# Two of eight K steps in the seven-product form, and GpSimd forming their sums of weights

## The chip, the cores and the metric

The kernel runs on one core of one Trainium2 chip. The metric is the device time of one launch in microseconds (us). An engine's name stands for its instruction stream: PE is TensorE, DVE is VectorE, ACT is ScalarE, POOL is GpSimd, SP is the queue that issues the loads.

## What is computed

One decoder block in float32 for 256 rows of 2048 columns: a projection, an mLSTM branch and a convolution branch, their gated merge, a residual, and then a feed-forward network (FFN) with its residual and a last norm. The change touches the FFN's first half:

```python
hf = rmsnorm(x, norm_ffn[l])
act = silu(einsum('bsd,df->bsf', hf, w_gate[l])) * einsum('bsd,df->bsf', hf, w_up[l])
x = x + einsum('bsf,fd->bsd', act, w_down[l])
```

`w_gate` and `w_up` are 2048 x 5632.

## The kernel before

Float32 accuracy on PE comes from splitting: each factor is a high part (ACT rounds it to fp32r) and a low part (DVE subtracts the high part from the raw value), and each product is three matmuls, high by high, low by high, high by low. One matmul has 128 x 128 stationary and 512 moving columns.

Weights pass through a ring: SP loads a chunk of 1 MB into one of 4 slots of `w_raw`; ACT writes `w_hi` (2 slots), DVE writes `w_lo` (2 slots), PE multiplies. SP reloads a slot when DVE has written the `w_lo` of the chunk four back (`lo_split`). ACT may write `w_hi` of chunk c when PE has ended the high products of chunk c-2 (`hi_used`); DVE may write `w_lo` when PE has ended chunk c-2 (`lo_used`).

**The FFN's gate and up** (`ffn_turn`, `pair_step`, `pair_split`) run over 11 blocks of 512 columns, one turn each. A turn has 8 K steps. A step takes four 128 x 512 tiles of weights, two of gate and two of up, which lie two K tiles apart, and two row blocks by two K tiles of the normed x. A plain step (small "s" in `STEPS`) is 8 products, 24 matmuls. A step in the seven-product form (capital "S"), a Strassen-like scheme, is 7 products, 21 matmuls, and needs three sums of weights beside the raw ones and sums of x tiles. The sums of x (`form_raw`, `form_hi`, `form_lo`) are made once, by `forms` on DVE; the sums of weights are made in each S step:

```python
V.tensor_tensor(t_raw[:, 0:2, :], raw[:, 0:1, :].to_broadcast([P, 2, COLS]), raw[:, 1:3, :], ALU.add)
V.tensor_tensor(raw[:, 0, :], t_raw[:, 0, :], raw[:, 2, :], ALU.add)
V.tensor_tensor(t_raw[:, 2, :], raw[:, 0, :], raw[:, 3, :], ALU.add)
```

(L1146, L1149, L1151). Then ACT makes `t_hi` (128 x 1536) and `w_hi` (the second sum lies in the raw slot, so `w_hi` waits for it too), DVE makes `t_lo` (L1153) and `w_lo` (L858). `t_raw`, `t_hi` and `t_lo` have one buffer each.

The order is written out by hand in each engine's stream. During step j ACT and DVE prepare step j+1 (`pair_split(j + 1)`); the preparation of the next turn's step 0 comes in step 7. Steps 0 and 7 need both parts at their start, since they go bank by bank; the others need `w_lo` after their high products. At `LAST_S` three PSUM banks are complete: ACT copies one (`c_gate`), DVE adds the others (L1224, L1226). After step 7's `pair_split` DVE runs five adds from PSUM (L1235), ACT two silus (L779), DVE two multiplications (L1249); `turn_act` transposes the result after steps 1 and 2 of the next turn, and ACT copies it out (`act_taken`). In turn 0 some work is extra: the last block of x is transposed, split (`f_high`, `f_low`) and made into sums.

In the stage before, the output projection, `forms(0, ...)` is made in its last block's step q = 1, and the first S step's sums in q = 3. `form_raw0` lies where `t_raw` lies, so the sums of weights wait for `form_lo`. After the FFN's 11 turns comes the down projection (L1668 to L1675).

GpSimd has little to do before: constants, copies of heads (L452, L454), and reciprocal roots in two operations each, with a pow (L430, L433).

Of the kernel before, what the change touches and what calls it, by code (L numbers as in the profile page):

```python
# [29 lines left out]
ALU = mybir.AluOpType  # L30
# [5 lines left out]
P = 128  # L36
# [44 lines left out]
def hybrid_block(nc, x, norm_mix, w_in, b_igate, b_fgate, conv_w, mh_norm, w_branch_a, w_branch_b,  # L81
# [51 lines left out]
    with ExitStack() as ctx:  # L133
# [36 lines left out]
        x1 = at("x1", [P, RT, D], F32, R2 + AT)  # L170
        FORMS = 22
        HALF_CH = 3 * COLS * 4
# [51 lines left out]
        f_raw[3] = at("f_raw3", [P, KB, SEQ], F32, Z + 2 * AT)  # L224
        form_raw1 = at("form_raw1", [P, 10, P], F32, Z)

# [186 lines left out]
        def _(pool):  # L413
# [48 lines left out]
            pool.wait_ge(h_squared, RT * H)  # L462
            rstd_of(h_mean, ss[:], ss[:], rstd[:], 1, DV, h_rstd)
            pool.wait_ge(x1_summed, 1)
            rstd_of(x1_mean, sums[:], sums[:], r_x[:, 1, :], 1, D, x1_rstd)
            for r in range(RT):
                pool.wait_ge(y_total, r + 1)
                rstd_of(y_mean, sums[:, r:r + 1], ssx[:, 1, r:r + 1], r_x[:, 0, r:r + 1], r + 1, D, y_rstd)

        @block.scalar  # L470
        def _(act):
# [258 lines left out]

            def f_high(b, turned, halves=1):

                for h in range(halves):
                    act.wait_ge(f_turned, turned + h)
                    ks = range(h * KB // halves, (h + 1) * KB // halves)
                    src = bank_kt(4) if halves == 1 else ps[:, B_FREE, :].rearrange("p (k t) -> p k t", k=2)
                    for k in ks:
                        c = V_FN + b * KB + k
                        last = copy(f_raw[b][:, k, :], src[:, k - ks[0], :], scale=vecT[:, c:c + 1])
                    last.then_inc(f_raw_done, 1)  # L740
                    act.wait_ge(f_raw_done, turned + h)
                    copy(fT_hi[:, b * KB + ks[0]:b * KB + ks[-1] + 1, :],
                         f_raw[b][:, ks[0]:ks[-1] + 1, :]).then_inc(f_hi_done, 1)

            def forms_high(g, raw, at_form, count):
                act.wait_ge(form_step, 5 * (g + 1))
                copy(form_hi[:, at_form:at_form + count, :], raw[:]).then_inc(form_hi_done, 1)

            for n in range(NB):
                for q in range(BC):  # L750
                    c = Chunk(G_OUT + n * BC + q)
                    if n == NB - 1 and q == BC - 1:
                        pair_split(0, 0)
# [28 lines left out]
            def ffn_turn(i, last=False):  # L782
                first = starts(i)
                for j in range(2 * BC):
                    if j < 2 * BC - 1:
                        pair_split(j + 1, i)
                    elif last:
                        split(Chunk(G_DOWN))
                    else:
                        pair_split(0, i + 1)  # L790
                    if j == 0:
                        if first:
                            f_high(NB - 1, NB, halves=2)
# [11 lines left out]
                    if last and j == LAST_S + 1:  # L805
# [44 lines left out]
        def _(dve):  # L850
# [279 lines left out]

            raw_units = w_raw[:].rearrange("p s (u n) -> p s u n", u=4)

            def pair_split(j, i):
# [12 lines left out]
                V.tensor_tensor(t_raw[:, 0:2, :], raw[:, 0:1, :].to_broadcast([P, 2, COLS]), raw[:, 1:3, :],  # L1146
                                ALU.add).then_inc(t_step, 1)
                dve.wait_ge(t_step, before * T_STEPS + 1)
                V.tensor_tensor(raw[:, 0, :], t_raw[:, 0, :], raw[:, 2, :], ALU.add).then_inc(t_step, 1)  # L1149
                dve.wait_ge(t_step, before * T_STEPS + 2)  # L1150
                V.tensor_tensor(t_raw[:, 2, :], raw[:, 0, :], raw[:, 3, :], ALU.add).then_inc(t_step, 1)  # L1151
                dve.wait_ge(t_hi_done, before + 1)
# [32 lines left out]
            for n in range(NB):  # L1185
                for q in range(BC):
# [18 lines left out]
            def ffn_turn(i, last=False):  # L1205
                first = starts(i)
                for j in range(2 * BC):
# [98 lines left out]
        def _(pe):  # L1306
# [262 lines left out]
            def tile_of(part, c, name):  # L1569
# [192 lines left out]
```

## Time and profile before

| | us |
|---|---|
| median of 2 runs | 1812.46 (1812.35 to 1812.58) |
| the profiled execution | 1813.08 |
| its span in the trace | 1811.3 |
| PE busy in it | 1750.6 |
| DVE busy | 1056.2 |
| ACT busy | 807.3 |
| POOL busy | 31.1 |

The profiled execution is 0.6 us above the median, and its span is 1.8 us short of its own time (launch and end). A busy share is an average over the stages; the FFN's gate and up lie between 1025 and 1560 us of the span.

### The profile page before, as it was taken

The numbers are of one execution on the slowest core, as the hardware profiler recorded it, in microseconds if no ns is written. First come the engines' busy times: TensorE is split into PE (matmuls) and PEld (weight loads), VectorE is DVE, ScalarE is ACT, GpSimd is POOL, SyncE is SP. The second block draws the span as 40 slices with busy tenths as digits, with TensorE's granted clock in tenths as the row PEclk, the third lists the DMA queues.
The fourth block names the chain that finished last, engine by engine and source line by source line (L and its number), as shares of the span: only waits on it lengthen the run. The fifth ranks groups of instructions, "written<-read, shape, count | busy, mean of one in ns | idle before, by whom it ended". The sixth has DMA issues, their size and how long they took to land.

```text
span 1811.3 us, 21190 instructions
## 1 busy us (share of the span) xinstructions
PE 1750.6 (97%) x7784; PEld 1441.7 (80%) x7784; DVE 1056.2 (58%) x862; ACT 807.3 (45%) x717; POOL 31.1 (2%) x43
## 2 busy tenths in 40 slices
PE   9999999999999999999999889999999999999997
PEld 8888888888888888888888667777777777788886
DVE  5454445655565544444445587777777777654455
ACT  6344445454444433333335444444444444544444
POOL 1000010110000000000000000000000000000000
PEclk9999999999999999999999999999999999999999
DMA  8656555555565555565665345555545555655552
GB/s 288 199 165 200 167 177 168 173 163 185 162 205 188 188 186 192 179 208 174 201 238 188 128 149 176 185 175 173 173 162 174 185 180 170 226 189 188 201 190 93
DMA packets 152106, 331.09 MB, mean 183 GB/s; under 512 B 8736, under 2 KB 8832, under 8 KB 146048
## 3 DMA queue, kind: packets, MB, share of 16 engines
q1 hardware_dynamic: 152064, 330.51, 55.0%
q8 instruction: 29, 0.48, 0.1%
q14 instruction: 13, 0.11, 0.0%
HBM read 328.38 MB, written 2.10 MB: 182 GB/s over the span
## 4 chain that ended last, share of the span: by engine, by line
PE 77%; DVE 8%; ACT 7%; issue 7%; DVEq 0%; ACTq 0%; DMA 0%; POOL 0%; SPq 0%; POOLq 0%
PE ps L1321 17%; PE ps L1322 17%; PE ps L1330 17%; ACT w_hi L472 7%; PE ps L1668 4%; PE ps L1675 4%; PE ps L1670 4%; PE ps L1598 3%; PE ps L1599 3%; PE ps L1603 3%; DVE w_lo L858 3%; DVE t_raw L1146 2%; DVE w_raw L1149 1%; DVE t_raw L1151 1%; PE ps L1339 1%
## 5 line engine op out<-in xcount | busy, mean ns | idle before, releaser
L858 DVE TENSOR_TENSOR w_lo<-w_raw,w_hi 128x2048 fp32r<-128x2048 f32 x308 | 706.7, 2299 | 469.6 <-ACT w_hi L472 466.0
L472 ACT ACTIVATE w_hi<-w_raw 128x2048 fp32r<-128x2048 f32 (+1 forms) x309 | 587.5, 1907 | 383.6 <-PE ps L1322 214.0
L1321 PE MATMUL ps<-w_hi,xT_hi 128*128 128x512 f32 x1024 | 404.4, 395 | 0.0
L1322 PE MATMUL ps<-w_hi,xT_lo 128*128 128x512 f32 x1024 | 398.7, 389 | 0.0
L1330 PE MATMUL ps<-w_lo,xT_hi 128*128 128x512 f32 x1024 | 253.0, 389 | 0.0
L1330 PEld LDWEIGHTS ps<-w_lo,xT_hi 128*128 128x128 f32 x1024 | 192.2, 188 | 39.9
L1321 PEld LDWEIGHTS ps<-w_hi,xT_hi 128*128 128x128 f32 x1024 | 192.3, 188 | 39.7
L1322 PEld LDWEIGHTS ps<-w_hi,xT_lo 128*128 128x128 f32 x1024 | 192.3, 188 | 39.0
L1598 PE MATMUL ps<-w_hi,fT_hi 128*128 128x512 f32 x396 | 162.3, 410 | 47.1 <-DVE w_lo L858 30.9
L1599 PE MATMUL ps<-w_hi,fT_lo 128*128 128x512 f32 x396 | 157.6, 398 | 0.0
L1598 PEld LDWEIGHTS ps<-w_hi,fT_hi 128*128 128x128 f32 x396 | 75.9, 192 | 71.5 <-issue 49.5
L1603 PE MATMUL ps<-w_lo,fT_hi 128*128 128x512 f32 x396 | 122.8, 396 | 0.0
L472 ACT ACTIVATE t_hi<-t_raw 128x1536 fp32r<-128x1536 f32 x33 | 49.2, 1489 | 116.7 <-DVE t_raw L1151 115.5
L1668 PE MATMUL ps<-w_hi,a_hi 128*128 128x512 f32 x352 | 96.1, 390 | 0.7 <-ACT actT L472 0.7
L1670 PE MATMUL ps<-w_hi,a_lo 128*128 128x512 f32 x352 | 95.9, 389 | 0.0
L1675 PE MATMUL ps<-w_lo,a_hi 128*128 128x512 f32 x352 | 88.9, 390 | 0.0
L1153 DVE TENSOR_TENSOR t_lo<-t_raw,t_hi 128x1536 fp32r<-128x1536 f32 x33 | 58.0, 1758 | 52.8 <-ACT t_hi L472 52.8
L1603 PEld LDWEIGHTS ps<-w_lo,fT_hi 128*128 128x128 f32 x396 | 75.9, 192 | 16.1
L1599 PEld LDWEIGHTS ps<-w_hi,fT_lo 128*128 128x128 f32 x396 | 76.3, 193 | 14.3
L1668 PEld LDWEIGHTS ps<-w_hi,a_hi 128*128 128x128 f32 x352 | 66.0, 188 | 14.9 <-ACT actT L472 0.9
L1675 PEld LDWEIGHTS ps<-w_lo,a_hi 128*128 128x128 f32 x352 | 66.0, 188 | 14.1 <-DVE w_lo L858 0.5
L1670 PEld LDWEIGHTS ps<-w_hi,a_lo 128*128 128x128 f32 x352 | 66.0, 188 | 13.7
(220 smaller groups left out, 1792.2 us busy)
## 6 DMA issues: line engine op xcount, KB each, us to landing
w_raw<-in_w_in SPq DMA_DIRECT2D x127, 1024.0 KB, 5.5
w_raw<-in_w_gate SPq DMA_DIRECT2D x88, 512.0 KB, 3.6
w_raw<-in_w_up SPq DMA_DIRECT2D x88, 512.0 KB, 4.4
w_raw<-in_w_down SPq DMA_DIRECT2D x44, 1024.0 KB, 4.8
w_raw<-in_w_branch_a SPq DMA_DIRECT2D x16, 1024.0 KB, 5.1
w_raw<-in_w_branch_b SPq DMA_DIRECT2D x16, 1024.0 KB, 5.0
w_raw<-in_w_out SPq DMA_DIRECT2D x16, 1024.0 KB, 5.2
xn<-in_x SPq DMA_DIRECT2D x4, 512.0 KB, 8.4
```

The costliest lines, as they stand in the source:

```text
L472: copy = lambda o, i, **kw: nc.scalar.activation(o, i, ACT.Copy, **kw)
L858: V.tensor_tensor(w_lo[:, chunk.split, :], w_raw[:, chunk.raw, :], w_hi[:, chunk.split, :].bitcast(F32), ALU.subtract).then_inc(lo_split, 1)
L1153: V.tensor_tensor(t_lo[:], t_raw[:].rearrange("p u n -> p (u n)"), t_hi[:].bitcast(F32), ALU.subtract).then_inc(t_lo_done, 1)
L1321: T.matmul(ps[:, banks + r, :], rows(hi, k, r), w, start=(q == 0 and k == 0), stop=False)
L1322: last = T.matmul(ps[:, banks + r, :], rows(lo, k, r), w, start=False, stop=False)
L1330: last = T.matmul(ps[:, banks + r, :], rows(hi, k, r), w, start=False, stop=(q == BC - 1 and k == KB - 1))
L1598: T.matmul(ps[:, bank, :], tile_of(0, k, name), moving(0, u), start=start, stop=False)
L1599: return T.matmul(ps[:, bank, :], tile_of(1, k, name), moving(0, u), start=False, stop=False)
L1603: return T.matmul(ps[:, bank, :], tile_of(0, k, name), moving(1, u), start=False, stop=stop)
L1668: T.matmul(ps[:, 4 * r + n, :], tile(h, r), cols_of(w_hi, n), start=start, stop=False)
L1670: ins = T.matmul(ps[:, 4 * r + n, :], tile(l, r), cols_of(w_hi, n), start=False, stop=False)
L1675: ins = T.matmul(ps[:, 4 * r + n, :], tile(h, r), cols_of(w_lo, n), start=False, stop=stop)
```

## The change

`STEPS` has two S steps, 0 and 3, where there were three, 0, 3 and 5. K pairs 4 and 5 keep their natural order. The three sums of weights move from DVE to POOL, into a loop that runs over the S steps by itself and waits for the landed pair and for the `t_lo` of the S step before. For x, the second group needs no S1, S2 and S4 forms, so `forms(1, ...)` makes 8 tiles and not 10; the split of the forms is a function of its own, one step later than the sums, for both groups. In turn 0 the two halves of the last block are split in steps 0 and 1, and not both in step 0. `LAST_S` is 3: ACT's copy of `c_gate` comes in step 3 and DVE's two adds in step 4.

```diff
-STEPS = "SssSsSss"
-PAIR_OF = (0, 2, 3, 1, 5, 4, 6, 7)
-LAST_S = 5
+STEPS = "SssSssss"
+PAIR_OF = (0, 2, 3, 1, 4, 5, 6, 7)
+LAST_S = 3
@@ POOL
+            def weight_sums(j, i):
+                c = Chunk(G_FFN + j, i, 2 * BC)
+                before = S_BEFORE[j] + i * S_TURNS
+                raw = raw_units[:, c.raw]
+                pool.wait_ge(pair_landed[c.raw], 32 * (j // RAW_SLOTS + 1) + i * 64)
+                if starts(i) and j == 0:
+                    pool.wait_ge(form_lo_done, 1)
+                else:
+                    pool.wait_ge(t_lo_done, before)
+                nc.gpsimd.tensor_tensor(out=t_raw[:, 0:2, :], in0=raw[:, 0:1, :].to_broadcast([P, 2, COLS]),
+                                        in1=raw[:, 1:3, :], op=ALU.add).then_inc(t_step, 1)
+                pool.wait_ge(t_step, before * T_STEPS + 1)
+                nc.gpsimd.tensor_tensor(out=raw[:, 0, :], in0=t_raw[:, 0, :], in1=raw[:, 2, :],
+                                        op=ALU.add).then_inc(t_step, 1)
+                pool.wait_ge(t_step, before * T_STEPS + 2)
+                nc.gpsimd.tensor_tensor(out=t_raw[:, 2, :], in0=raw[:, 0, :], in1=raw[:, 3, :],
+                                        op=ALU.add).then_inc(t_step, 1)
+            weight_sums(0, 0)
             pool.wait_ge(x1_summed, 1)
             rstd_of(x1_mean, sums[:], sums[:], r_x[:, 1, :], 1, D, x1_rstd)
+            weight_sums(LAST_S, 0)
+            with pool.Fori(1, FB) as i:
+                for j in (0, LAST_S):
+                    weight_sums(j, i)
@@ ACT
-                    if n == NB - 1 and q == 1:
+                    if n == NB - 1 and q == 2:
                         forms_high(0, form_raw0, 0, 12)
...
-                    if j == 0:
-                        if first:
-                            f_high(NB - 1, NB, halves=2)
-                        else:
-                            silu(i - 1, 1)
+                    if first and j in (0, 1):
+                        f_high(NB - 1, NB, 2, j)
+                    if not first and j == 0:
+                        silu(i - 1, 1)
...
-                        forms_high(1, form_raw1, 12, 10)
+                        forms_high(1, form_raw1, 12, 8)
@@ DVE, pair_split
-                raw = raw_units[:, c.raw]
-                dve.wait_ge(pair_landed[c.raw], 32 * (j // RAW_SLOTS + 1) + i * 64)
-                if starts(i) and j == 0:
-                    dve.wait_ge(form_lo_done, 1)
-                else:
-                    dve.wait_ge(t_lo_done, before)
-                V.tensor_tensor(t_raw[:, 0:2, :], ...)
-                V.tensor_tensor(raw[:, 0, :], ...)
-                V.tensor_tensor(t_raw[:, 2, :], ...)
                 dve.wait_ge(t_hi_done, before + 1)
@@ DVE, streams
                     if n == NB - 1 and q == 1:
-                        forms(0, form_raw0, 0, 2)
+                        forms(0, form_raw0, 2)
+                    if n == NB - 1 and q == 2:
+                        forms_low(0, form_raw0, 0, 12)
...
-                        f_low(NB - 1, NB, halves=2)
+                    if first and j in (0, 1):
+                        f_low(NB - 1, NB, 2, j)
+                    if first and j == 1:
+                        forms(1, form_raw1, KB)
                     if first and j == 2:
-                        forms(1, form_raw1, 12, 3)
-                    if j == LAST_S:
+                        forms_low(1, form_raw1, 12, 8)
+                    if j == LAST_S + 1:
                         dve.wait_ge(p1_out, i + 1)
```

## Rows read from the trace of the kernel before

**Rows 1.** The page's part 1: busy time, share and instructions of each engine.

```profile
PE 1750.6 (97%) x7784; PEld 1441.7 (80%) x7784; DVE 1056.2 (58%) x862; ACT 807.3 (45%) x717; POOL 31.1 (2%) x43
```

**Rows 2.** Windows: stretch, length, busy of PE, PEld, DVE, ACT, POOL; PEclk, DMA, GB/s.

```profile
1200.00:1300.00 100.00, 93.24 (x402) 75.59 (x402) 76.61 (x60) 45.42 (x33) 0.00 (x0) 0.97 0.52 178
...
1600.00:1700.00 100.00, 100.00 (x443) 82.81 (x442) 48.84 (x37) 42.79 (x38) 0.00 (x0) 1.00 0.55 196
```

**Rows 3.** Timeline, PE: first matmuls of turns 0, 1, 4 and 10, then the down projection's.

```profile
1025.16 0.77 PE L1598 MATMUL ps<-w_hi,fT_hi 128*128 128x512 f32 x1 [4.91 <-DVE w_lo L858]
...
1084.11 0.49 PE L1598 MATMUL ps<-w_hi,fT_hi 128*128 128x512 f32 x1 [2.37 <-DVE w_lo L858]
...
1228.16 0.79 PE L1598 MATMUL ps<-w_hi,fT_hi 128*128 128x512 f32 x1 [2.63 <-DVE w_lo L858]
...
1515.19 0.79 PE L1598 MATMUL ps<-w_hi,fT_hi 128*128 128x512 f32 x1 [2.63 <-DVE w_lo L858]
...
1560.01 0.61 PE L1668 MATMUL ps<-w_hi,a_hi 128*128 128x512 f32 x2
```

**Rows 4.** Timeline, PE: after step 0 of turn 0; first matmuls of two following steps.

```profile
1032.32 0.60 PE L1559 MATMUL ps<-ident,x 128*128 128x128 f32 x4
1032.67 0.48 PE L1598 MATMUL ps<-w_hi,fT_hi 128*128 128x512 f32 x1
...
1214.49 0.39 PE L1598 MATMUL ps<-w_hi,fT_hi 128*128 128x512 f32 x1
...
1219.93 0.39 PE L1598 MATMUL ps<-w_hi,fT_hi 128*128 128x512 f32 x1
```

**Rows 5.** Timeline: `c_gate`'s copy, then the preparation of turn 4's step 0.

```profile
1214.77 0.60 ACT L472 ACTIVATE c_gate<-ps 128x512 f32<-128x512 f32 x1 [3.51 <-PE ps L1603]
...
1222.21 1.49 ACT L472 ACTIVATE t_hi<-t_raw 128x1536 fp32r<-128x1536 f32 x1 [5.04 <-DVE t_raw L1151]
...
1223.60 1.90 ACT L472 ACTIVATE w_hi<-w_raw 128x2048 fp32r<-128x2048 f32 x1
1223.73 1.76 DVE L1153 TENSOR_TENSOR t_lo<-t_raw,t_hi 128x1536 fp32r<-128x1536 f32 x1 [1.64 <-ACT t_hi L472]
...
1225.62 2.29 DVE L858 TENSOR_TENSOR w_lo<-w_raw,w_hi 128x2048 fp32r<-128x2048 f32 x1
```

**Rows 6.** Groups of instructions, 1025 to 1560 us: count, busy us, mean ns, idle before.

```profile
L858 DVE TENSOR_TENSOR w_lo<-w_raw,w_hi 128x2048 fp32r<-128x2048 f32 x89 | 203.0, 2291 | 47.5 <-ACT w_hi L472 45.2
...
L1146 DVE TENSOR_TENSOR t_raw<-w_raw 128x1024 f32<-128x1024 f32 x32 | 39.0, 1219 | 0.0
...
L1149 DVE TENSOR_TENSOR w_raw<-t_raw,w_raw 128x512 f32<-128x512 f32 x32 | 22.2, 693 | 1.1
...
L1235 DVE TENSOR_TENSOR c_up<-ps,c_up 128x512 f32<-128x512 f32 x22 | 15.0, 682 | 0.0
L1249 DVE SCALAR_TENSOR_TENSOR c_up<-c_up,r_x,c_gate 128x512 f32<-128x512 f32 x20 | 15.0, 748 | 3.6 <-ACT c_gate L779 3.6
```

**Rows 7.** Groups of instructions, POOL, whole span: the pow of 16 columns.

```profile
L433 POOL TENSOR_TENSOR rstd<-ss,half 128x16 f32<-128x16 f32 x1 | 2.9, 2916 | 0.1
```

**Rows 8.** Timeline, DVE and then POOL, around 244 us.

```profile
244.37 2.59 DVE L858 TENSOR_TENSOR w_lo<-w_raw,w_hi 128x2048 fp32r<-128x2048 f32 x1 [0.35 <-ACT w_hi L472]
...
244.21 0.61 POOL L452 COPY head_qk<-qk 128x512 f32 x1 [49.93 <-DVE vx L1008]
244.76 2.26 POOL L454 COPY head_cols<-cols 128x6 f32 x1
```

**Rows 9.** The page's DMA issues: KB each, median us from issue to landing.

```profile
w_raw<-in_w_up SPq DMA_DIRECT2D x88, 512.0 KB, 4.4
```

**Rows 10.** Timeline: the end of the output projection, before turn 0.

```profile
1011.18 1.49 ACT L472 ACTIVATE form_hi<-form_raw 128x1536 fp32r<-128x1536 f32 x1 [4.30 <-DVE form_raw L1178]
...
1012.70 1.76 DVE L1181 TENSOR_TENSOR form_lo<-form_raw,form_hi 128x1536 fp32r<-128x1536 f32 x1 [1.55 <-ACT form_hi L472]
...
1014.52 0.50 PE L1321 MATMUL ps<-w_hi,mT_hi 128*128 128x512 f32 x1 [1.23 <-ACT w_hi L472]
```

More of the change, by code:

```diff
@@ L170, in hybrid_block @@
         x1 = at("x1", [P, RT, D], F32, R2 + AT)
-        FORMS = 22
+        FORMS = 20
         HALF_CH = 3 * COLS * 4
@@ L224, in hybrid_block @@
         f_raw[3] = at("f_raw3", [P, KB, SEQ], F32, Z + 2 * AT)
-        form_raw1 = at("form_raw1", [P, 10, P], F32, Z)
+        form_raw1 = at("form_raw1", [P, 8, P], F32, Z)
         g_final = at("g_final", [P, D], F32, R3)
@@ L309, in hybrid_block @@
         T_STEPS = 3
+        FORM_STEPS = (0, 5, 7)
         F_BLOCKS = NB - 1
@@ L463, in _ @@
             rstd_of(h_mean, ss[:], ss[:], rstd[:], 1, DV, h_rstd)
+            raw_units = w_raw[:].rearrange("p s (u n) -> p s u n", u=4)
+            def weight_sums(j, i):
[16 more added lines that the diff above has]
+            weight_sums(0, 0)
             pool.wait_ge(x1_summed, 1)
             rstd_of(x1_mean, sums[:], sums[:], r_x[:, 1, :], 1, D, x1_rstd)
+            weight_sums(LAST_S, 0)
+            with pool.Fori(1, FB) as i:
+                for j in (0, LAST_S):
+                    weight_sums(j, i)
             for r in range(RT):
@@ L729, in pair_split, with f_high @@
                 split(c, (t_step, before * T_STEPS + T_STEPS))
-            def f_high(b, turned, halves=1):
-                for h in range(halves):
+            def f_high(b, turned, halves=1, at_half=0):
+                for h in (range(at_half, at_half + 1) if halves > 1 else (0,)):
                     act.wait_ge(f_turned, turned + h)
@@ L745, in forms_high @@
             def forms_high(g, raw, at_form, count):
-                act.wait_ge(form_step, 5 * (g + 1))
+                act.wait_ge(form_step, FORM_STEPS[g + 1])
                 copy(form_hi[:, at_form:at_form + count, :], raw[:]).then_inc(form_hi_done, 1)
@@ L804, in ffn_turn @@
                         copy(c_gate[:, 0, :], ps[:, B_P1, :]).then_inc(p1_out, 1)
-                    if last and j == LAST_S + 1:
+                    if last and j == LAST_S + 2:
                         stage(Chunk(G_DOWN))
@@ L1128, in _ @@
                 merge_turn(i)
-            raw_units = w_raw[:].rearrange("p s (u n) -> p s u n", u=4)
             def pair_split(j, i):
@@ L1139, in pair_split @@
                 before = S_BEFORE[j] + i * S_TURNS
-                raw = raw_units[:, c.raw]
-                dve.wait_ge(pair_landed[c.raw], 32 * (j // RAW_SLOTS + 1) + i * 64)
-                if starts(i) and j == 0:
-                    dve.wait_ge(form_lo_done, 1)
-                else:
-                    dve.wait_ge(t_lo_done, before)
[L1146 to L1151, printed above, removed]
                 dve.wait_ge(t_hi_done, before + 1)
@@ L1155, in pair_split, with f_low @@
                 split(c)
-            def f_low(b, done, halves=1):
-                for h in range(halves):
+            def f_low(b, done, halves=1, at_half=0):
+                for h in (range(at_half, at_half + 1) if halves > 1 else (0,)):
                     dve.wait_ge(f_hi_done, done + h)
@@ L1163, in f_low, with forms @@
                                     ALU.subtract).then_inc(f_lo_done, 1)
-            def forms(g, raw, at_form, plain):
+            def forms(g, raw, plain):
                 a, b = f_raw[g], f_raw[g + 2]
@@ L1170, in forms, with forms_low @@
                 top, low = slice(0, P), slice(P, 2 * P)
-                V.tensor_tensor(s1, a[:, 0:sums, low], b[:, 0:sums, low], ALU.subtract).then_inc(form_step, 1)
+                if sums:
+                    V.tensor_tensor(s1, a[:, 0:sums, low], b[:, 0:sums, low], ALU.subtract).then_inc(form_step, 1)
                 V.tensor_tensor(raw[:, 0:KB, :], a[:, :, top], a[:, :, low], ALU.subtract).then_inc(form_step, 1)
-                dve.wait_ge(form_step, 5 * g + 1)
-                V.tensor_tensor(s2, s1, a[:, 0:sums, top], ALU.subtract).then_inc(form_step, 1)
+                if sums:
+                    dve.wait_ge(form_step, FORM_STEPS[g] + 1)
+                    V.tensor_tensor(s2, s1, a[:, 0:sums, top], ALU.subtract).then_inc(form_step, 1)
                 V.tensor_tensor(raw[:, KB:KB + plain, :], b[:, sums:, top], b[:, sums:, low],
                                 ALU.subtract).then_inc(form_step, 1)
-                dve.wait_ge(form_step, 5 * g + 3)
-                V.tensor_tensor(s4, s2, b[:, 0:sums, top], ALU.add).then_inc(form_step, 1)
+                if sums:
+                    dve.wait_ge(form_step, FORM_STEPS[g] + 3)
+                    V.tensor_tensor(s4, s2, b[:, 0:sums, top], ALU.add).then_inc(form_step, 1)
+            def forms_low(g, raw, at_form, count):
                 dve.wait_ge(form_hi_done, g + 1)
-                count = KB + plain + 3 * sums
                 V.tensor_tensor(form_lo[:, at_form:at_form + count, :], raw[:],
@@ L1226, in ffn_turn @@
                         V.tensor_tensor(c_gate[:, 1, :], ps[:, B_P7, :], c_up[:, 0, :], ALU.add).then_inc(u_step, 1)
-                    if last and j == LAST_S + 1:
+                    if last and j == LAST_S + 2:
                         stage(Chunk(G_DOWN))
@@ L1575, in tile_of @@
                 g, k = c // KB, c % KB
-                plain = (2, 3)[g]
+                plain = (2, 4)[g]
                 sums = KB - plain
```

## Prediction

> **What bounds the kernel now.** I read the page's shares first: PE is busy for 97% of the span [rows 1], so time can be won only where PE waits or runs slowly. The windows say where: in the down projection 100 us hold 443 matmuls at a granted clock of 1.00; in the FFN's gate and up, 402 at 0.97 [rows 2]. Then the timeline of PE, for the turns. Turn 0 takes 1084.11 - 1025.16 = 58.95 us, turns 1 to 9 take (1515.19 - 1084.11) / 9 = 47.90 us each, turn 10 takes 1560.01 - 1515.19 = 44.82 us [rows 3].
>
> Against this, PE's own pace: a plain step of 24 matmuls takes 1219.93 - 1214.49 = 5.44 us, 0.2267 us a matmul [rows 4]. An S step is then 4.76 us. Transposes between two steps cost about 0.5 us: 0.35 until the next step starts, the rest in its long first matmul [rows 4]. A turn of before holds 3 x 21 + 5 x 24 = 183 matmuls: 41.5 + 1.0 = 42.5 us. So some 5.4 us of each 47.90 are lost. The reader sees where in rows 3 and 5: PE stands 2.63 us at the turn's start, for a `w_lo` that is the last of a serial chain. DVE forms three sums (1.22 + 0.69 + 0.69) [rows 6], ACT makes `t_hi`, then `w_hi`, DVE `t_lo` and at last `w_lo`. DVE does the sums only after the `w_lo` before, and ACT idles 5.04 us for them [rows 5]. The remainder is a second short stall at the other S steps and the clock, which after the turn's stall is granted at its lower level, 1.2 in place of 2.4 GHz; step 0 of turn 0, behind 4.91 us of idleness, took 1032.32 - 1025.16 = 7.16 us and not 4.76 [rows 3, 4].
>
> **PE's new work.** One S step becomes plain: 3 matmuls more a turn, 0.68 us, 7.5 us over 11 turns. All of it is on the path. A turn's floor is 186 x 0.2267 + 1.0 = 43.17 us.
>
> **What leaves DVE.** Nine additions a turn (3 x 2.6 = 7.8 us) and one `t_lo` (1.76). ACT loses one `t_hi` (1.49). Left on DVE are 8 x 2.29 + 2 x 1.76 + 5 x 0.68 + 2 x 0.69 + 2 x 0.75 = 28.1 us of 43.17 [rows 5, 6].
>
> **What comes to POOL.** Two-input adds of 1024, 512 and 512 columns, twice a turn. No row shows one. From below, DVE's 2.6 us for a step. The nearest row of POOL is a copy of 512 columns, 0.61 us [rows 8]; 2048 columns are 2.4 us with one input, 4.9 with two read one after the other. The only two-input rows are pows, 2.9 us for 16 columns [rows 7], which as a rate would make a step over 300 us; it is a different operation, and the copy is nearest in size and kind. I take 4.9 us (2.45 + 1.2 + 1.2).
>
> What POOL does also takes from DVE. A copy of POOL runs from 244.21 to 244.82 [rows 8], and the `w_lo` that starts in it takes 2.59 and not 2.29 us; the tiny copy behind it, 6 columns, lasts 2.26 us and ends at 247.02, with that `w_lo` at 246.96. So the two exclude each other, an instruction at a time. The Trainium skill says the same (SBUF — State Buffer, section on the two separate sides): the pair of ports is an exclusive lock between a GpSimd operation and a DVE one with two SBUF inputs, and the first to start holds it. By that rule the L1235 adds, with one input in PSUM, go free. Its GPSIMD Engine Reference (section 3.1) gives 4497 ns for a two-input add of 2048 columns and advises DVE for such adds; by it a step is an estimated 4.8 us, and the sum below stays.
>
> **Does the new chain fit in 43.17 us?** Time 0 is the start of a turn's step 0 on PE. Steps start at 0, 4.76, 10.70, 16.64, 21.40, 26.84, 32.28, 37.72, and the next turn's at 43.17.
> - ACT copies `c_gate` at 21.4 (0.60) [rows 5]. `w_lo`(4) waits for `w_hi`(4), which comes behind the transposed result's copy at 16.7, and ends at 21.5. SP then issues the load of the next step 0; gate's and up's issue take some 0.6 us, and up lands 4.4 later [rows 9], at 26.5.
> - POOL's first add: 26.6 to 29.05. `w_lo`(6), ready at 27.8, waits for it and ends at 31.35. The second add then to 32.65, `w_lo`(7) to 34.95, the third add to 36.2.
> - `t_hi` 36.3 to 37.8, `t_lo` to 39.75, `w_hi` to 39.6, `w_lo`(next 0) 39.8 to 42.1. PE wants it at 43.17: 1.05 us to spare.
> - The load of step 3's pair is issued at 35.1 and lands at 40.0; POOL waits for the `w_lo` under way, then adds from 42.15 to about 47.5, between DVE's two multiplications. The next `w_lo`(1) ends about 50.5, 7.3 after the new turn's start, and is wanted at 4.76 + 3.63 = 8.4. One us to spare.
> - What is queued behind POOL's waits: only its own later sums and, in turn 0, the reciprocal root, in which DVE's and ACT's last steps of turn 0 take an interest, 40 us later.
>
> So the gain rests on about 1 us of cover in two places. Gone that, each us late costs one us a turn.
>
> **Entry and turn 0.** The forms' split one step later frees ACT for `w_hi` of the output projection's last chunk, and the 1.23 us stall at 1014.52 goes [rows 10]. But DVE now does that chunk's `w_lo` first (1011.15 to 1013.4), then `form_lo` to 1015.2; POOL adds 1015.3 to 1020.2 and the chain of rows 5 follows: `t_hi` to 21.8, `t_lo` to 23.6, `w_lo` to 26.0. Turn 0 starts at 1026.1 and not 1025.16: +0.95. In turn 0 the split of the second half no longer stands ahead of `w_hi`(2); `w_hi`(3) ends at 44.8 for a start at 45.2, `form_lo` at 48.7 for one at 50. I find no stall, so 43.17 + 2.4 (low clock in step 0) = 45.57.
>
> **The sum**
> - entry: +0.95
> - turn 0: 45.57 - 58.95 = -13.4
> - turns 1 to 9: 9 x (43.17 - 47.90) = -42.6
> - turn 10: 43.17 - 44.82 = -1.65
> - all: -56.7 us. Profiled execution 1813.08 to 1756.4; on the median of 1812.46, 1755.8. I say 1756.
>
> With POOL at DVE's price only the entry moves, by -2.3: 1753.5.
>
> **Rivals**
> 1. *POOL takes the lock before the turn's last `w_lo`.* Step 3's adds are released by `t_lo` (39.75) and the landing (40.0), `w_lo` is ready at 39.8. If the pair lands a few tenths sooner, POOL may be first; `w_lo` ends at 42.2 + 2.3 = 44.6, 1.5 us late, in ten turns 15: 1771. For: 0.2 us between the two. Against: DVE follows itself at once.
> 2. *POOL also holds up DVE's adds from PSUM.* No row excludes it. Adds and POOL's would alternate from 42.1 on: the three adds that free the first two shared banks end near 49.0, PE wants the second of these banks at 43.17 + 12 x 0.2267 = 45.9. Some 3 us a turn, 30 in all: 1786. The Trainium skill's lock rule, quoted above, speaks against this one.
> 3. *POOL's two-input add is slow, and the kernel slower.* The chain above allows x <= 6.1 us for a step's sums (43.17 - 26.6 - 4.6 of two `w_lo` - 5.9 of the chain after). Above, each us is a us a turn: 8.1 gives 1776, 10.8 brings back 47.9, from 15.4 on the kernel is over 2% slower. At 16 us (2.0 for 512 columns of one input, over three times the copy's): 1756 + 10 x 9.9 = 1855. For: the pow of rows 7. Against: the copy of rows 8.
>
> **How the numbers follow.** Forecast (1750 to 1764) 0.52; rival 1 (1764 to 1776) 0.22; rival 2 (1776 to 1795) 0.14; POOL so slow, or a chain of late steps, that time ends between 1776 and 1849 by other ways 0.08; rival 3 above 1849 0.04. A change of 2%, 36 us, is about what a measurement of this kernel can tell from none. Faster by over 2% is below 1776: 0.52 + 0.22 + 0.02 for the low side of the others = 0.76. Slower 0.04, same 0.20. Range: 1750, below POOL's lower bound, to 1782, the lower part of rival 2. The likeliest case's own range is 1750 to 1764.
>
> **What the profile after would show.** Turn starts 43.2 us apart, without the 2.63 us stall; granted clock 0.99 or 1.00 in this stage; POOL at some 22 x 4.9 = 108 us plus what it waits in the lock; `w_lo` with a mean above 2.29 us, up to 3.5 for the ones behind POOL. Turn starts 44.7 apart with a wait for `w_lo` is rival 1; a wait for `c_step`'s adds, with L1235 longer than 0.68, is rival 2; ACT's `t_hi` waiting for POOL past 38 us of the turn is rival 3. I am wrong most cheaply in the price of POOL's add and in the order in which the lock is granted.

## The result and the profile after

| | before | changed |
|---|---|---|
| median, us | 1812.46 | 1755.84 (1755.32 to 1756.35) |
| profiled execution, us | 1813.08 | 1755.32 |
| its span, us | 1811.3 | 1753.5 |

The ratio is 0.9688, with a 95% interval of 0.9665 to 0.9712. A second set of runs gave 1756.33 and 0.9685 (0.9669 to 0.9701). So the change saves 3.1%, and the prediction's 1756 and its 56.7 us stand.

The page's part 1 of the changed kernel answers to [rows 1]:

```profile
PE 1732.6 (99%) x7817; PEld 1434.9 (82%) x7817; DVE 995.3 (57%) x749; ACT 794.2 (45%) x706; POOL 173.3 (10%) x109
```

Two windows of the changed kernel, with the columns of [rows 2], lie in the FFN's gate and up, and the last in the down projection:

```profile
1200.00:1300.00 100.00, 100.00 (x453) 82.73 (x452) 70.78 (x44) 48.73 (x36) 32.00 (x15) 1.00 0.57 196
1300.00:1400.00 100.00, 100.00 (x452) 82.79 (x451) 72.38 (x44) 50.08 (x36) 24.91 (x13) 1.00 0.55 189
...
1600.00:1700.00 100.00, 100.00 (x443) 82.81 (x442) 47.28 (x36) 43.50 (x37) 0.00 (x0) 1.00 0.53 193
```

There are 33 more matmuls and yet 18 us less of PE busy time: at the higher clock they take less, and 100 us of the gate and up now hold some 452 matmuls at a granted clock of 1.00, where there were 402 at 0.97. The timeline of PE of the changed kernel shows the starts of turns 0 and 1 and of the down projection (it answers to [rows 3]), and the end of step 0 of turn 0:

```profile
1025.76 0.76 PE L1619 MATMUL ps<-w_hi,fT_hi 128*128 128x512 f32 x1 [7.30 <-DVE w_lo L884]
...
1032.04 0.60 PE L1580 MATMUL ps<-ident,x 128*128 128x128 f32 x4
...
1070.95 0.39 PE L1619 MATMUL ps<-w_hi,fT_hi 128*128 128x512 f32 x1
...
1502.21 0.61 PE L1689 MATMUL ps<-w_hi,a_hi 128*128 128x512 f32 x2
```

Turn 0 takes 45.19 us, the ten others (1502.21 - 1070.95) / 10 = 43.13. The one long stall left in this stage is the first, 7.30 us.

One turn's start in POOL's and then DVE's timeline (turn 5 starts on PE at 1243.45). The first three POOL rows are the sums for its step 0, the last three those for its step 3. L884 is `w_lo`, L1165 `t_lo`, L1256 the adds from PSUM, L1270 the two multiplications:

```profile
1227.28 2.40 POOL L477 TENSOR_TENSOR t_raw<-w_raw 128x1024 f32<-128x1024 f32 x1 [23.37 <-DMA w_raw<-in_w_up]
1229.76 3.23 POOL L480 TENSOR_TENSOR w_raw<-t_raw,w_raw 128x512 f32<-128x512 f32 x1
1233.07 3.29 POOL L483 TENSOR_TENSOR t_raw<-w_raw 128x512 f32<-128x512 f32 x1
1240.36 4.18 POOL L477 TENSOR_TENSOR t_raw<-w_raw 128x1024 f32<-128x1024 f32 x1 [4.00 <-DMA w_raw<-in_w_up]
1244.62 1.28 POOL L480 TENSOR_TENSOR w_raw<-t_raw,w_raw 128x512 f32<-128x512 f32 x1
1245.98 1.62 POOL L483 TENSOR_TENSOR t_raw<-w_raw 128x512 f32<-128x512 f32 x1
...
1227.94 3.88 DVE L884 TENSOR_TENSOR w_lo<-w_raw,w_hi 128x2048 fp32r<-128x2048 f32 x1
1232.91 2.29 DVE L884 TENSOR_TENSOR w_lo<-w_raw,w_hi 128x2048 fp32r<-128x2048 f32 x1 [1.09 <-ACT w_hi L499]
1238.08 1.76 DVE L1165 TENSOR_TENSOR t_lo<-t_raw,t_hi 128x1536 fp32r<-128x1536 f32 x1 [2.88 <-ACT t_hi L499]
1239.97 2.29 DVE L884 TENSOR_TENSOR w_lo<-w_raw,w_hi 128x2048 fp32r<-128x2048 f32 x1
...
1244.58 0.68 DVE L1256 TENSOR_TENSOR c_gate<-ps,c_gate 128x512 f32<-128x512 f32 x1
1245.18 2.98 DVE L1270 SCALAR_TENSOR_TENSOR c_up<-c_up,r_x,c_gate 128x512 f32<-128x512 f32 x2
```

The exclusion of [rows 8] is at work in most of these rows. POOL's first add ends at 1229.68, and the `w_lo` that began beside it needs 3.88 us, until 1231.82. POOL's second add needs 3.23, since it waits for that `w_lo`; the third needs 3.29, since it waits for the `w_lo` of 1232.91. But the L1256 add, which reads PSUM and one SBUF tile, keeps its 0.68 us beside the POOL add of 1244.62. A length in these rows contains the wait for the other engine. Free of it, POOL's adds take 2.40 and 1.28 us. The chain ends when `w_lo` of step 0 does, at 1242.26, 1.19 us before PE wants it.

This turn is one of the two tight ones in this trace. In the other eight POOL's third add starts a few hundredths ahead of `w_lo`(7), and not behind it; `w_lo` of step 0 then ends 2.72 us before PE wants it. So it is for turn 4, which starts on PE at 1200.33 (POOL, then DVE):

```profile
1189.73 1.29 POOL L483 TENSOR_TENSOR t_raw<-w_raw 128x512 f32<-128x512 f32 x1
1189.78 3.38 DVE L884 TENSOR_TENSOR w_lo<-w_raw,w_hi 128x2048 fp32r<-128x2048 f32 x1 [1.29 <-ACT w_hi L499]
...
1195.32 2.29 DVE L884 TENSOR_TENSOR w_lo<-w_raw,w_hi 128x2048 fp32r<-128x2048 f32 x1 [0.48 <-ACT w_hi L499]
```

In the trace of `changed_again`, the same kernel, all ten turns are of the tight kind, with 0.98 to 1.19 us to spare. Either way a turn takes 43.13 us.

### The profile page after: what moved, and what is told of

Read it like the earlier page. It is cut to its first block, busy times and chain, and to the rows that moved or that the text cites. A ratio compares the mean times of both kernels' runs of the same rounds, so it can differ in the third digit from the quotient of the medians.

```text
span 1753.5 us, 21136 instructions
## 1 busy us (share of the span) xinstructions
PE 1732.6 (99%) x7817; PEld 1434.9 (82%) x7817; DVE 995.3 (57%) x749; ACT 794.2 (45%) x706; POOL 173.3 (10%) x109
## 4 chain that ended last, share of the span: by engine, by line
PE 96%; DVE 1%; POOL 1%; ACT 1%; issue 0%; DMA 0%; SPq 0%; DVEq 0%; POOLq 0%; ACTq 0%
PE ps L1342 18%; PE ps L1343 18%; PE ps L1351 18%; PE ps L1619 9%; PE ps L1620 9%; PE ps L1624 9%; PE ps L1689 4%; PE ps L1696 4%; PE ps L1691 4%; PE ps L1360 1%; PE ps L1580 1%; ACT w_hi L499 0%; DVE w_lo L884 0%; POOL t_raw L477 0%; DMA w_raw<-in_w_in 0%
## 5 line engine op out<-in xcount | busy, mean ns | idle before, releaser
L884 DVE TENSOR_TENSOR w_lo<-w_raw,w_hi 128x2048 fp32r<-128x2048 f32 x308 | 732.8, 2381 | 500.9 <-ACT w_hi L499 498.9
L1619 PE MATMUL ps<-w_hi,fT_hi 128*128 128x512 f32 x440 | 173.8, 395 | 7.6 <-DVE w_lo L884 7.3
L1620 PE MATMUL ps<-w_hi,fT_lo 128*128 128x512 f32 x440 | 171.7, 390 | 0.0
L477 POOL TENSOR_TENSOR t_raw<-w_raw 128x1024 f32<-128x1024 f32 x22 | 56.1, 2552 | 821.4 <-DVE form_lo L1197 532.8
L1624 PE MATMUL ps<-w_lo,fT_hi 128*128 128x512 f32 x440 | 130.4, 390 | 0.0
L1619 PEld LDWEIGHTS ps<-w_hi,fT_hi 128*128 128x128 f32 x440 | 82.7, 188 | 24.8 <-issue 7.7
L1624 PEld LDWEIGHTS ps<-w_lo,fT_hi 128*128 128x128 f32 x440 | 82.7, 188 | 17.2
L1620 PEld LDWEIGHTS ps<-w_hi,fT_lo 128*128 128x128 f32 x440 | 82.8, 188 | 16.5
L1619 PE MATMUL ps<-w_hi,form_hi 128*128 128x512 f32 x176 | 68.9, 391 | 0.0
```

The source lines that it names most:

```text
L477: nc.gpsimd.tensor_tensor(out=t_raw[:, 0:2, :], in0=raw[:, 0:1, :].to_broadcast([P, 2, COLS]), in1=raw[:, 1:3, :], op=ALU.add).then_inc(t_ ...
L884: V.tensor_tensor(w_lo[:, chunk.split, :], w_raw[:, chunk.raw, :], w_hi[:, chunk.split, :].bitcast(F32), ALU.subtract).then_inc(lo_split, 1)
L1619: T.matmul(ps[:, bank, :], tile_of(0, k, name), moving(0, u), start=start, stop=False)
L1620: return T.matmul(ps[:, bank, :], tile_of(1, k, name), moving(0, u), start=False, stop=False)
L1624: return T.matmul(ps[:, bank, :], tile_of(0, k, name), moving(1, u), start=False, stop=stop)
```

## Experiments

**Who forms the sums, and where the last S step stands.** Four kernels with two S steps (the changed kernel is one of them): sums on DVE or POOL, second S step at 3 or at 5. And one with only half the change, three S steps with POOL.

`two_s_dve`, against the changed kernel:

```diff
@@ DVE, pair_split
+                V.tensor_tensor(t_raw[:, 0:2, :], raw[:, 0:1, :].to_broadcast([P, 2, COLS]), raw[:, 1:3, :], ALU.add)
+                V.tensor_tensor(raw[:, 0, :], t_raw[:, 0, :], raw[:, 2, :], ALU.add)
+                V.tensor_tensor(t_raw[:, 2, :], raw[:, 0, :], raw[:, 3, :], ALU.add)
                 dve.wait_ge(t_hi_done, before + 1)
@@ POOL
-            weight_sums(0, 0)
...
```

> The changed kernel with its two S steps, but DVE forms the sums of weights as before (2.6 us a step). Theory A (what made the old chain late was ACT's copy of c_gate at step 5, which held w_hi(7) back, and the S step there; POOL is not needed): w_lo(7) ends at 34.8 of the turn, sums to 37.5, t_hi to 39.1, t_lo to 41.0, w_lo(next 0) to 43.3 against a start wanted at 43.17, so 0 to 0.3 us of stall a turn, and the entry 2.3 us shorter: 1753 to 1759. Rival B (the move to POOL carries the gain): a stall of 2 us or more at each turn's start with the low clock behind it, some 3 us a turn: 1780 to 1790.

Measured: 1764.91 us, ratio 0.9732 (0.9716 to 0.9748). Theory A's mechanism, not its size. Turns 1 to 10 take 43.57 us on average, 0.44 above the changed kernel's, 4.4 us together. The entry, counted from the first of the `forms` additions, is 2.4 us shorter, as expected. The miss is in turn 0, which I had not looked at: it takes 51.70 us and not 45.19. In its timeline PE waits 3.95 us before step 3, since ACT's `t_hi` waits 4.55 us for sums which stand in DVE's stream behind `f_low` and `forms`, and eleven matmuls after that wait start 0.43 us apart.

```profile
1024.29 0.47 PE L1608 MATMUL ps<-w_hi,fT_hi 128*128 128x512 f32 x1 [4.85 <-DVE w_lo L859]
1046.72 0.79 PE L1608 MATMUL ps<-w_hi,fT_hi 128*128 128x512 f32 x1 [3.95 <-ACT w_hi L474]
```

`late_s_dve` and `late_s_pool`, against `two_s_dve` and the changed kernel:

```diff
-STEPS = "SssSssss"
-PAIR_OF = (0, 2, 3, 1, 4, 5, 6, 7)
-LAST_S = 3
+STEPS = "SssssSss"
+PAIR_OF = (0, 2, 3, 4, 5, 1, 6, 7)
+LAST_S = 5
@@ PE, turn 0: the second group's forms are wanted a step sooner
-                    if first and j == KB:
+                    if first and j == KB - 1:
```

> As two_s_dve (two S steps, DVE forms the sums), but the second S step is step 5 and LAST_S is 5, as in the kernel before; the K pairs 1, 4 and 5 change places for it. Same matmuls as the changed kernel. Theory A (the old turn start was late because ACT's copy of c_gate at the end of step 5 stands ahead of w_hi(7)): w_hi(7) ends at 34.7 and not 32.4 of the turn, w_lo(next 0) at 45.6, 2.4 us late, and the low clock behind it, 4 us a turn more than two_s_dve: 1795 to 1810. Rival (the gain of two_s_dve came from fewer sums on DVE as such): as two_s_dve, 1762 to 1770.

> The changed kernel (POOL forms the sums) with the second S step at 5 in the same way. Theory A: the sums are ready on POOL before the late w_hi(7) is, so the chain after it is only t_hi, t_lo and w_lo, and ends 0.5 to 1 us ahead: 1756 to 1764. So POOL takes away the harm of the late copy, and moving the copy takes away the need of POOL. Rival (the lock makes POOL's sums late): a stall at the turn's start, 1775 or more.

Measured: `late_s_dve` 1819.06 us, ratio 1.0033 (1.0020 to 1.0045), about the time of the kernel before. `late_s_pool` 1762.59 us, ratio 0.9723 (0.9707 to 0.9739). The timeline of `late_s_dve` (ACT, DVE, PE) shows a chain like the old one:

```profile
1208.54 0.60 ACT L474 ACTIVATE c_gate<-ps 128x512 f32<-128x512 f32 x1 [3.51 <-PE ps L1613]
1209.03 1.91 ACT L474 ACTIVATE w_hi<-w_raw 128x2048 fp32r<-128x2048 f32 x1
...
1210.97 2.29 DVE L859 TENSOR_TENSOR w_lo<-w_raw,w_hi 128x2048 fp32r<-128x2048 f32 x1 [3.22 <-ACT w_hi L474]
1213.18 0.68 DVE L1234 TENSOR_TENSOR c_up<-ps,c_gate 128x512 f32<-128x512 f32 x1
1213.90 0.69 DVE L1236 TENSOR_TENSOR c_gate<-ps,c_up 128x512 f32<-128x512 f32 x1
1214.51 1.22 DVE L1147 TENSOR_TENSOR t_raw<-w_raw 128x1024 f32<-128x1024 f32 x1
...
1223.18 0.77 PE L1608 MATMUL ps<-w_hi,fT_hi 128*128 128x512 f32 x1 [3.88 <-DVE w_lo L859]
```

ACT waits 3.51 us for step 5's end to copy `c_gate`, and `w_hi`(7) stands behind that copy; then `w_lo`(7), two adds and only then the sums. PE waits 3.88 us at each turn's start, and turns 1 to 9 take 49.5 us on average. That is 9 us more than the top of my range, in which I had left out the two adds between `w_lo`(7) and the sums: from the end of `w_lo`(7), 1213.26, to the sums at 1214.51 they cost 1.25 us a turn.

These two adds are not in the old chain. In the kernel before they come at step `LAST_S` itself, while ACT makes `w_hi`(7); the changed kernel has them at `LAST_S` + 1, and `late_s_dve` took that over. The kernel before, at the same place of turn 3:

```profile
1215.26 1.91 ACT L472 ACTIVATE w_hi<-w_raw 128x2048 fp32r<-128x2048 f32 x1
...
1215.49 0.70 DVE L1224 TENSOR_TENSOR c_up<-ps,c_gate 128x512 f32<-128x512 f32 x1 [1.51 <-ACT c_gate L472]
1216.22 0.69 DVE L1226 TENSOR_TENSOR c_gate<-ps,c_up 128x512 f32<-128x512 f32 x1
1217.21 2.29 DVE L858 TENSOR_TENSOR w_lo<-w_raw,w_hi 128x2048 fp32r<-128x2048 f32 x1 [0.29 <-ACT w_hi L472]
1219.41 1.22 DVE L1146 TENSOR_TENSOR t_raw<-w_raw 128x1024 f32<-128x1024 f32 x1
```

So of the 3.88 us of stall in `late_s_dve` some 1.25 are that kernel's own, and the rest is close to the 2.63 us of the kernel before. An estimate from these rows: with the two adds in their old place `late_s_dve` would be some 13 us faster, near 1806 us. No run shows it.

In `late_s_pool` a turn is 43.13 us, as in the changed kernel: POOL has the sums ready while `w_hi`(7) is late. Turn 0 takes 6.6 us more, 51.82: a 3.93 us stall before step 3, which the earlier want of the forms brings (the second group's `form_lo` ends at 1048.98, PE goes on at 1049.08), and the low clock behind it. So with two S steps each half of the remedy is nearly enough alone: the S step at 3 lets DVE do the sums, POOL makes the late S step harmless. Of the 63 us between 1819.1 and 1756.3 the one gives 54, the other 56; they don't add. By the estimate above some 13 us of each are the misplaced adds. The position of the S step, of the copy and of the two adds were moved together in these runs, so what the copy alone is worth was not measured. From the rows, `w_hi`(7) starts 14.15 us before the next turn does in `late_s_dve`, with 3.88 of stall in it, so 10.27 us before PE wants it; in `two_s_dve` it is 12.84 - 0.18 = 12.66 us. The late copy thus takes 2.4 us of the chain, and the adds 1.25: together nearly the 3.70 us by which the two stalls differ.

`three_s_pool`, against the kernel before: the three additions leave DVE's `pair_split`, and POOL has `weight_sums` with

```diff
+            weight_sums(0, 0)
...
+            for j in (3, 5):
+                weight_sums(j, 0)
+            with pool.Fori(1, FB) as i:
+                for j in (0, 3, 5):
+                    weight_sums(j, i)
```

> The kernel before with its three S steps and its LAST_S of 5; only the sums of weights move to POOL. Its PE floor is 42.5 us a turn. Theory A: POOL's adds come off DVE, w_lo(7) ends at 36.4, the sums by 36.3, w_lo(next 0) at about 42.0 of 42.5, so the turn is near its floor, 42.5 to 43.5; turn 0 keeps its long order (53 us or so) and the entry grows by 2.3 us: 1755 to 1767. Rival B (three S steps are too many for POOL with one t_raw and the lock): a turn of 44.5 us or more, 1775 and above.

Measured: 1785.86 us, ratio 0.9848 (0.9832 to 0.9865): rival B. A turn is 45.1 us. POOL's timeline, the sums of step 5 of one turn and of step 0 of the next:

```profile
1233.65 4.55 POOL L476 TENSOR_TENSOR t_raw<-w_raw 128x1024 f32<-128x1024 f32 x1 [9.86 <-DVE t_lo L1166]
1238.28 3.33 POOL L479 TENSOR_TENSOR w_raw<-t_raw,w_raw 128x512 f32<-128x512 f32 x1
1241.68 1.28 POOL L482 TENSOR_TENSOR t_raw<-w_raw 128x512 f32<-128x512 f32 x1
1246.44 4.50 POOL L476 TENSOR_TENSOR t_raw<-w_raw 128x1024 f32<-128x1024 f32 x1 [3.47 <-DVE t_lo L1166]
```

Before these two steps POOL waits for `t_lo`, that is for the single `t_raw`, and not for a landing as in the changed kernel. And the sums need 5 us alone, but take 9.3 in step 5 (two of the three adds wait in the lock), 11.3 in step 0 (all three) and 7.1 in step 3. With two S steps in the same late order (`late_s_pool`) a turn is at its floor, so it is the third S step that costs, by its wait for the buffer and its turns in the lock; the two were not told apart.

**How much cover there is.** POOL adds of 128x512 into a spare tile ahead of each step's sums; the results stay whole:

```diff
+                for m in range(N):
+                    nc.gpsimd.tensor_tensor(out=spare[:], in0=raw[:, 1, :], in1=raw[:, 3, :], op=ALU.add)
```

> One more POOL add of 128x512 ahead of each step's sums, 1.37 us. w_lo of step 0 has 1.2 us to spare in the changed kernel. Theory: 0.2 us late a turn if POOL doesn't take the lock before it, 1757 to 1760; with the lock's 1.1 us as in extra2, 1768 to 1772.

> The changed kernel with two more POOL adds of 128x512 into a spare tile ahead of each S step's sums: 2.7 us longer on POOL. In the trace of the changed kernel w_lo(0) ends 1.2 us before PE wants it. Theory (the sums on POOL lie on the chain, with about 1.2 us of cover): 1.5 us late a turn, 1768 to 1774. Rival (POOL is hidden, PE alone bounds): 1756.

> The same with four more POOL adds, 5.4 us longer. Theory: 4.2 us late a turn and the low clock after such a stall, 0 to 1.8 us more: 1798 to 1816, about the time of the kernel before. Rival (hidden): 1756.

Measured, one run each: 1772.02, 1801.83 and 1845.34 us. Turns 1 to 9 take 44.4, 47.1 and 50.9 us on average. That POOL lies on the chain is shown; that a us late costs a us is not: `extra2` and `extra4` came out 28 and 29 us above my ranges, and `extra1` reached its upper range in another way than the one I named (its `w_lo` of step 0 keeps its 2.29 us). With 1.37, 2.7 and 5.4 us more on POOL in each S step, a turn loses 1.3, 4.0 and 7.8 us.

In `extra1` most of it is lost at the second place of cover that the prediction names, the `w_lo` of step 1. Turn 4 starts at 1208.81; the low products of its step 1 come 9.16 us later, and not 8.39 as in the changed kernel:

```profile
1217.97 1.21 PE L1630 MATMUL ps<-w_lo,fT_hi 128*128 128x512 f32 x4 [0.52 <-DVE w_lo L890]
```

In `extra2` the first of POOL's step 3 adds comes into the lock just ahead of DVE's `w_lo` of step 0, on which PE waits (POOL, DVE, PE):

```profile
1265.38 4.59 POOL L481 TENSOR_TENSOR spare<-w_raw 128x512 f32<-128x512 f32 x2 [3.56 <-DVE t_lo L1171]
...
1265.44 3.38 DVE L890 TENSOR_TENSOR w_lo<-w_raw,w_hi 128x2048 fp32r<-128x2048 f32 x1
...
1268.91 0.47 PE L1625 MATMUL ps<-w_hi,fT_hi 128*128 128x512 f32 x1 [2.35 <-issue]
...
1269.72 0.63 PE L1625 MATMUL ps<-w_hi,form_hi 128*128 128x512 f32 x1
1270.15 0.63 PE L1626 MATMUL ps<-w_hi,form_lo 128*128 128x512 f32 x1
```

`w_lo` takes 3.38 us, 1.1 more than alone. That is rival 1 of the prediction, which the changed kernel misses by 0.39 us in the turn shown above (1239.97 against 1240.36). And after the 2.35 us of idleness matmuls start 0.43 us apart, and not 0.23, the clock's lower level, for eight or so.

`extra2_held` keeps POOL off that `w_lo`:

```diff
+                if j == LAST_S:
+                    pool.wait_ge(lo_split, Chunk(G_FFN, i, 2 * BC).count(1))
```

> As extra2 (1801.8 us), but POOL starts step 3's adds only after the w_lo of step 0, so that it can't take the lock ahead of that w_lo (which took 3.38 us in extra2, 1.1 more than alone). Theory: the chain ends 1.1 us sooner, 1.2 us late and not 2.35; 10 to 11 us less, and if so short a stall leaves the clock high, 19 more: 1770 to 1791. Rival (the lock isn't what stretched that w_lo, or PE's loss has another cause): 1798 to 1803.

Measured: 1809.32 us, 7.5 us more and not 10 less. The step that I tested is right and the sum is wrong. The first PE row is the start of turn 5, where the stall fell from 2.35 to 1.38 us, 0.97 less; that `w_lo` is back at 2.29. But POOL's adds now run later, and they and DVE's two multiplications (4.66 us for both, 1.5 alone) take turns in the lock; the next `w_lo`s are late, and in every turn from 1 to 9 a stall of 2.1 to 2.2 us stands at step 1's low products, where `extra2` has 1.85 us in turns 1 and 2 and at most 0.5 in the others:

```profile
1271.27 0.47 PE L1627 MATMUL ps<-w_hi,fT_hi 128*128 128x512 f32 x1 [1.38 <-issue]
1282.10 1.20 PE L1632 MATMUL ps<-w_lo,fT_hi 128*128 128x512 f32 x4 [2.17 <-DVE w_lo L892]
...
1274.08 4.66 DVE L1278 SCALAR_TENSOR_TENSOR c_up<-c_up,r_x,c_gate 128x512 f32<-128x512 f32 x2
1278.66 5.58 DVE L892 TENSOR_TENSOR w_lo<-w_raw,w_hi 128x2048 fp32r<-128x2048 f32 x2
```

**What the lock excludes.** A write-only operation of POOL behind the sums of turns 1 to 7:

```diff
+                    pool.memset(spare[:], 0.0)
```

> The changed kernel with one POOL memset of 128x2048 (1.8 us alone) behind each step's sums in turns 1 to 7, which reads nothing; its target is a part of actT not yet in use. It falls beside DVE's w_lo of step 1. Theory (the exclusion is between reads, so a write-only POOL operation runs beside DVE's w_lo): both keep their lengths, 1.80 and 2.29, time 1755 to 1757. Rival (any POOL operation excludes): w_lo or memset up to 1.8 longer.

Measured: 1755.79 us, one run. The memset that starts at 1248.03 runs until 1249.84; both keep their lengths (1.81, and 4.48 for two `w_lo`; of 14 memsets, seven of them beside a `w_lo`, the shortest took 1.80, the longest 1.82):

```profile
1248.03 1.81 POOL L494 MEMSET spare<- 128x2048 f32 x1
...
1248.57 4.48 DVE L889 TENSOR_TENSOR w_lo<-w_raw,w_hi 128x2048 fp32r<-128x2048 f32 x2
```

**The stall that is left.** `entry_early` moves `form_raw0` off `t_raw`, so that the first sums need no `form_lo`; `entry_early2` also forms turn 0's second sums ahead of the reciprocal root:

```diff
-form_raw0 = at("form_raw0", [P, 12, P], F32, s + 2 * HALF_CH)
+form_raw0 = at("form_raw0", [P, 12, P], F32, s + HALF_CH)
@@ POOL, first sums
-                    pool.wait_ge(form_lo_done, 1)
+                    pool.wait_ge(lo_used, G_OUT)
@@ DVE, pair_split
+                if starts(i) and j == 0:
+                    dve.wait_ge(form_lo_done, 1)
@@ POOL, entry_early2 only
             weight_sums(0, 0)
+            weight_sums(LAST_S, 0)
             pool.wait_ge(x1_summed, 1)
             rstd_of(x1_mean, sums[:], sums[:], r_x[:, 1, :], 1, D, x1_rstd)
-            weight_sums(LAST_S, 0)
```

> The changed kernel with form_raw0 moved from t_raw's place to t_lo's, so that POOL's first sums need not wait for form_lo. Theory: the chain at the FFN's entry loses POOL's 5 us, PE's stall of 7.3 us goes and with it the low clock of step 0 (2 us): 1746 to 1749. Rival (another wait takes its place, DVE's w_lo and form_lo in a row): 1752 to 1756.

> The changed kernel itself, beside the next one on one chip: 1755 to 1757, and the ratio to the kernel before within 0.967 to 0.971.

> As entry_early (1750.9 us), and POOL forms turn 0's second sums before the reciprocal root and not after it. In entry_early PE stood 2.17 us before step 3 of turn 0, for a w_hi behind a t_hi that waited 2.76 us for POOL, and about eight matmuls after it ran at half the pace (1.7 us). Theory: the sums start when their pair has landed, some 7 us sooner, and both go: 1746 to 1748. Rival (POOL's adds then hold up DVE's w_lo of steps 1 and 2 in the lock): 1750 or more.

Measured: `entry_early` 1750.86 us, ratio 0.9659 (0.9643 to 0.9675), `changed_again` 1756.33, `entry_early2` 1747.91, ratio 0.9636 (0.9620 to 0.9652). In `entry_early` the stall of 7.30 us fell to 0.42, but 2.17 us and a low clock came at step 3 of turn 0, and the gain was 5 us and not 8. `entry_early2` takes these too. Its timeline of PE has one stall in the FFN's start, of 0.42 us:

```profile
1021.06 0.47 PE L1621 MATMUL ps<-w_hi,fT_hi 128*128 128x512 f32 x1 [0.42 <-DVE w_lo L884]
```

Its window from 1000 to 1050 us, in the columns of [rows 2], has a granted clock of 1.00:

```profile
1000.00:1050.00 50.00, 49.58 (x226) 40.78 (x226) 36.70 (x28) 31.71 (x32) 14.72 (x9) 1.00 0.53 173
```

It is 8.4 us faster than the changed kernel on the same chip, and 3.6% faster than the kernel before.

## Why the prediction was right, and where it was not

- **The floor and the turn.** 43.17 us forecast, 43.13 measured over ten turns: with no stall and the clock high a turn is its 186 matmuls and two transposes. The plain step in place of the S step was priced at 0.68 us by the matmul; the sum bears it out, no run shows it by itself.
- **Turn 0.** 45.57 forecast, 45.19 measured. The term that was off is the low clock. The first step took 1032.04 - 1025.76 = 6.28 us, not the 7.16 I took over from before, behind an idle time that is longer, not shorter. The granted clock says why; windows of the kernel before, then of the changed one, in the columns of [rows 2]:

```profile
1022.00:1025.16 3.16, 0.00 (x0) 0.03 (x1) 3.12 (x3) 0.69 (x1) 0.00 (x0) 0.69 0.00 0
1025.16:1030.00 4.84, 4.84 (x12) 3.78 (x13) 1.50 (x2) 3.25 (x5) 0.00 (x0) 0.50 0.67 217
...
1022.00:1025.76 3.76, 0.00 (x1) 0.03 (x1) 3.72 (x3) 1.29 (x1) 0.00 (x0) 0.50 0.00 0
1025.76:1028.80 3.04, 3.04 (x7) 2.44 (x8) 0.98 (x1) 1.99 (x5) 0.00 (x0) 0.50 0.58 181
```

  In the changed kernel the clock has been at its lower level (0.50) for 3.76 us when the turn starts, so 3.04 us of matmuls fall into it; before it fell later in the idle time, and 4.84 us of matmuls fell into it. Half of each, 1.52 and 2.42 us, is what the two first steps lost against 4.76.
- **The entry.** +0.95 forecast. Turn 0 starts at 1025.76, 0.60 later than before, on a stream which was already 0.28 us ahead (the `forms` begin at 1008.84 and not 1009.12): +0.88. The 1.23 us stall at 1014.52 went, as forecast.
- **POOL's price.** 2.45 + 1.2 + 1.2 taken, 2.40 + 1.28 + 1.26 at its shortest. The copy, counted twice for two inputs, was the right row, though nothing of before showed that a second input doubles the price. POOL is busy for 142 us with the 22 steps, 6.5 us a step: 1.5 are the waits in the lock, which the forecast of 108 us left open.
- **The lock and its two places of cover.** 1.05 us to spare forecast for `w_lo` of step 0; 1.19 in the turn shown, 2.72 in eight of the ten, 0.98 to 1.19 in `changed_again`. What decides is whether `w_lo`(7) or POOL's third add comes first, a near tie that I had not seen; I had the tight case. In the turn shown the stations of my timeline hold within 0.5 us: POOL's first add starts at 26.96 (26.6 forecast), `t_hi` at 36.2 (36.3), `w_lo` of step 0 at 39.65 (39.8). The other place, `w_lo` of step 1, ends at 1250.35 and is wanted at 1251.84: 1.5, where I had 1.0. DVE keeps the lock for the `w_lo` of step 0 (1239.97 against 1240.36; in the eight other turns POOL's add comes later still), so rival 1 did not come; `extra2` shows that it can, and its price of about 1 us and a low clock.
- **Rival 2** is refuted by the L1256 row: adds from PSUM go free. So the Trainium skill's rule (SBUF — State Buffer, section on the two separate sides), that the lock is between a GpSimd operation which reads SBUF and a DVE one with two SBUF inputs, agrees with all three cases here: two inputs wait (3.88 for 2.29), one input does not (0.68), a memset does not (1.81).
- **What failed**, though the result did not hang on it: "each us late costs one us a turn", and with it rival 3's scale. I had 6.1 us as free for a step's sums and 10.8 as break-even. With 6.3 us (`extra1`) a turn already lost 1.3, where that rule gives 0.2, and with 10.4 (`extra4`) the kernel was 32 us slower than before. Two things that the rule leaves out are in the rows: the second place of cover, at step 1, gives way too, and after 2.35 us of idleness, in `extra2`, the low clock adds its own loss. That every POOL operation more is also one more exchange of the lock fits, but was not tested by itself.
- **What I had not seen** is why the old chain was late. I named its members; that the copy of `c_gate` at step 5 stands in front of `w_hi`(7), and that this is worth 2.4 us of the chain, only the four kernels with two S steps showed. My timeline had it in the right place without my knowing what that was worth: that part of the forecast is luck. So the title's two parts are not two gains that add: two S steps with DVE's sums save 49 us (1813.74 to 1764.91), POOL's sums with three S steps 28 (1813.74 to 1785.86), both 57.

The Trainium skill's advice to leave elementwise adds to DVE (GPSIMD Engine Reference, section 3.1) is right in price, 2.40 against 1.22 us for 1024 columns. It does not decide here, where DVE stands on the chain and POOL has nothing to do: 1756.3 against 1764.9, most of it in turn 0.

## What to carry to other kernels

Follow the chain that ends last back past its members to the instruction that stands in front of it in an in-order queue; here moving the last S step, with the copy and the adds behind it, two steps forward was worth about as much as an engine's help. When work goes to an engine that shares a lock with the busy one, lay both streams out over one period and state the slack at each place where a third engine waits: a slack of 1 us was enough, and 1.4 us more of work in each S step were too much. And after each stall that is removed look at the next one, turn 0 and entry included: they were another 8 us.

## What the hardware showed that I had not expected

- The lock goes to whoever starts first, also when that is by hundredths: in `extra2` POOL is first by 0.06 us and DVE waits; in turn 4 of the changed kernel by 0.05. Within 0.02 us the recorded starts don't tell who has it: in `extra1` DVE's `w_lo` starts at 1250.75, POOL's add at 1250.76 and waits (3.44 us for 1.29); in `three_s_pool` POOL's add is recorded first, by 0.007 us, and still waits (3.44), while `w_lo` keeps its 2.28.
- Three POOL adds of 5.0 us became 9.3 where two of them met a DVE instruction, and 11.3 where all three did, in the steps of `three_s_pool`. The loser waits until the other's instruction has ended.
- The stall ahead of turn 0 grew from 4.91 to 7.30 us, and the slow step behind it became shorter by 0.88 us, since more of the low clock passed in idle time.
